# Fourteen of 32 gate panels of a decoder layer moved from between the attention's steps to a stretch of their own ahead of it

## What is computed

```
h    = rmsnorm(x)
proj = h @ w_in          # split into q, kv, nsa_g, u, v, merge_g
o_a  = nsa_attention(q, compressed / selected / window keys and values, sigmoid(nsa_g))
o_b  = spatial_gating(gelu(u), gelu(v), ...)
g    = sigmoid(merge_g)                        # 2 x 2048 columns
merged = g[0] * (o_a @ w_proj_a) + g[1] * (o_b @ w_proj_b)
x    = x + merged @ w_mix_out
```

## Time and profile before

| | us |
|---|---|
| median of 2 runs | 2777.32 |
| lowest and highest | 2776.36, 2778.28 |
| span of the profiled execution | 2772.1 |
| first product of `sv` in it | 810.28 |

### The profile page before, as it was taken

The page is one execution under the profiler, slowest core; times in us unless marked ns, Lnnn a source line. Parts: engine busy times, 40 slices in busy tenths (PEclk is TensorE's granted clock), DMA queues, the critical chain, the costliest instruction groups (busy, mean ns, idle before and its releaser), DMA issues.

```text
span 2772.1 us, 37764 instructions
## 1 busy us (share of the span) xinstructions
PE 2737.9 (99%) x14015; PEld 2313.9 (83%) x14015; DVE 2050.9 (74%) x3133; ACT 1083.8 (39%) x1831; POOL 442.5 (16%) x406
## 2 busy tenths in 40 slices
PE   8999999999999999999999999999999999999998
PEld 7888788888888888888877888888888888788886
DVE  7544476776655555555678899999999999988887
ACT  6201254444420322211144555555555555443334
POOL 0200133343320445511000000000000000010000
PEclk9999999999999999999999999999999999999999
DMA  8532323322233444544334788888888888899882
GB/s 248 165 93 74 86 77 96 96 77 81 80 110 91 108 135 136 155 114 114 110 115 127 187 198 213 213 205 211 208 219 201 215 198 260 290 307 302 289 269 95
DMA packets 610806, 455.19 MB, mean 164 GB/s; under 512 B 13669, under 2 KB 555225, under 8 KB 604761
## 3 DMA queue, kind: packets, MB, share of 16 engines
q1 hardware_dynamic: 551328, 405.97, 49.3%
q0 software_dynamic: 46416, 30.41, 8.2%
q10 hardware_dynamic: 12904, 16.71, 1.9%
HBM read 394.06 MB, written 58.98 MB: 163 GB/s over the span
## 4 chain that ended last, share of the span: by engine, by line
PE 85%; DVE 6%; ACT 3%; issue 2%; DMA 2%; POOL 1%; ACTq 0%; DVEq 0%; SPq 0%; POOLq 0%
PE banks L893 12%; PE banks L894 12%; PE banks L895 12%; PE banks L1293 9%; PE banks L1290 9%; PE banks L1291 9%; PE banks L1355 4%; PE banks L1357 4%; PE banks L1356 4%; PE banks L1062 1%; PE banks L1121 1%; PE banks L1123 1%; PE banks L1122 1%; PE banks L1093 1%; PE banks L1078 1%
## 5 line engine op out<-in xcount | busy, mean ns | idle before, releaser
L1372 DVE CAST w_hi<-raw 128x512 fp32r<-128x512 f32 x424 | 229.1, 540 | 357.6 <-PE banks L895 292.7
L893 PE MATMUL banks<-act_hi,w_hi 128*128 128x512 f32 (+1 forms) x1232 | 489.3, 397 | 0.0
L894 PE MATMUL banks<-act_lo,w_hi 128*128 128x512 f32 (+1 forms) x1232 | 481.1, 390 | 0.0
L895 PE MATMUL banks<-act_hi,w_lo 128*128 128x512 f32 (+1 forms) x1232 | 481.0, 390 | 0.0
L1374 DVE TENSOR_TENSOR w_lo<-raw,w_hi 128x512 fp32r<-128x512 f32 x424 | 314.2, 741 | 14.6
L1291 PEld LDWEIGHTS banks<-t_hl,wf_lo 128*128 128x128 f32 x1312 | 246.5, 188 | 58.3
L895 PEld LDWEIGHTS banks<-act_hi,w_lo 128*128 128x128 f32 (+1 forms) x1232 | 230.2, 187 | 51.3
L893 PEld LDWEIGHTS banks<-act_hi,w_hi 128*128 128x128 f32 (+1 forms) x1232 | 230.7, 187 | 40.7 <-DVE w_lo L1374 0.6
L894 PEld LDWEIGHTS banks<-act_lo,w_hi 128*128 128x128 f32 (+1 forms) x1232 | 230.9, 187 | 39.4
L1293 PE MATMUL banks<-t_hl,wf_hi 128*128 128x512 f32 x656 | 259.4, 396 | 0.0
L1290 PE MATMUL banks<-t_hl,wf_hi 128*128 128x512 f32 x656 | 259.2, 395 | 0.0
(11 more groups left out here) (323 smaller groups left out, 5351.8 us busy)
## 6 DMA issues: line engine op xcount, KB each, us to landing
raw_f<-in_w_ffn_in_dram SPq DMA_DIRECT2D x82, 1024.0 KB, 8.9
raw<-in_w_in_dram SPq DMA_DIRECT2D x68, 1024.0 KB, 5.6
h_full<-hidden_blocks SPq DMA_DIRECT2D x35, 1024.0 KB, 8.1
wo_raw<-in_w_ffn_out_dram SPq DMA_DIRECT2D x32, 1024.0 KB, 10.1
hidden_blocks<-tok_hl SPq DMA_DIRECT2D x44, 512.0 KB, 6.2
s<-in_w_ffn_in_dram SPq DMA_DIRECT2D x40, 512.0 KB, 5.9
s<-in_w_ffn_in_dram POOLq DMA_DIRECT2D x40, 512.0 KB, 6.5
raw<-in_w_mix_out_dram SPq DMA_DIRECT2D x16, 1024.0 KB, 6.1
```

Of the source, the lines that this page charges most:

```text
L893: pe.matmul(dst, w_hi[:, q, j, 0:m], hi, start=first, stop=False)
L894: pe.matmul(dst, w_hi[:, q, j, 0:m], lo, start=False, stop=False)
L895: return pe.matmul(dst, w_lo[:, q, j, 0:m], hi, start=False, stop=last)
L1372: dve.tensor_copy(w_hi[:, q, :, 0:width], src).then_inc(hi_done, 1)
```

## The change

`plan()` gets a phase `m0` of 14 panels between `g` and `merge`, and `merge` keeps 18. PE does the 14 as plain groups, one panel after the other, with `turn_gates` behind the first; DVE splits them whole, with `value_low(3)` behind the first; ACT copies and stores them through the same two buffers `gate_out`. The planner now spreads 288 tiles over the same 128 steps: 38, 83, 68, 77 and 22. The order of the panels, of the stores and of all phases behind stays.

```diff
+EARLY_GATES = 14
...
-        ("merge", (32,)), ("sv", (8,)), ("su", (8,)), ("ab", (16, 4, 2, 2)), ("wo", (16,)),
+        ("m0", (EARLY_GATES,)), ("merge", (2 * DK - EARLY_GATES,)), ("sv", (8,)), ("su", (8,)), ("ab", (16, 4, 2, 2)), ("wo", (16,)),
...
-        GATE_TILES = 32 * DK
+        GATE_TILES = PH["merge"].n * DK
...
-            columns(PH["merge"], w_in_v, C_MERGE)
+            columns(PH["m0"], w_in_v, C_MERGE)
+            columns(PH["merge"], w_in_v, C_MERGE + EARLY_GATES * P)
...
+            ph = PH["m0"]
+            for n in range(ph.n):
+                group(ph, *ph.at(n), hi16, lo16)
+                if n == 0:
+                    turn_gates()
+
             ph = PH["merge"]
             def gate_tiles(tiles):
...
                 gate_tiles(tiles[:third])
-                if step == 0:
-                    turn_gates()
                 if step < ITEMS:
                     scores(step)
...
+            ph = PH["m0"]
+            for n in range(ph.n):
+                split(ph, *ph.at(n))
+                if n == 0:
+                    value_low(3)
             ph = PH["merge"]
             split(ph, 0, 0, quarters=range(AHEAD))
-            value_low(3)
...
                 for k in QUARTERS_AT[step]:
                     k += AHEAD
-                    split(PH["merge"] if k < 128 else PH["sv"], 0, k % 128 // 4, quarters=(k % 4,))
+                    p = k // 4
+                    if p < PH["merge"].n:
+                        split(PH["merge"], 0, p, quarters=(k % 4,))
+                    else:
+                        split(PH["sv"], 0, 0, quarters=(k % 4,))
...
+            def gates_out(ph, p, tile):
+                act.wait_ge(quarters_done, ph.quarter0 + 4 * p + 4)
+                wait(act, gate_stored[tile % 2], 16 * (tile // 2))
+                act.activation(gate_out[:, tile % 2], bank[(ph.group0 + p) % 2][:], ACT.Copy).then_inc(banks_read, 1)
+                act.wait_ge(banks_read, ph.group0 + p + 1)
+                act.dma_start(merge_dram[tile * P:(tile + 1) * P, :], gate_out[:, tile % 2]).then_inc(gate_stored[tile % 2], 16)
+            for p in range(EARLY_GATES):
+                gates_out(PH["m0"], p, p)
+
             ph = PH["merge"]
...
                     if k % 4 == 3:
-                        p = k // 4
...
+                        gates_out(ph, k // 4, EARLY_GATES + k // 4)
```

## The result

The changed kernel takes 2839.36 us (2838.66 to 2840.07, 2 runs) against 2777.32 us before: a ratio of 1.0228, 95% interval 1.0198 to 1.0257. It is slower; whether by more than 2% is just not certain, since the interval starts at 1.0198. The forecast was 2836 us, in a range of 2823 to 2857. The profiled execution spans 2836.9 us against 2772.1, 64.8 us more.

A forecast was written before the change was run, and what follows sets the result against it. PE's work was taken to bound the kernel before; after the change DVE's loop would make PE stand 59 us, with 0 from the other parts. 2777.3 + 59 = 2836 us, range 2823 to 2857.

The forecast's parts named there:

- The plain stretch: Ahead of the attention, from about 319 us: fourteen panels at 10.84 us each, 152 us at PE's own time.
- Rival D: The plain stretch stalls on loads or the banks' copies: 14 us more, 2850; counted within the sum's 0.80.
- The loop on DVE: In the four scoring windows DVE needs 374.8 us against PE's 315.9, so PE stands 58.9 us.
- The price of a quarter: One weight quarter in DVE's loop: 1.06, say 1.07 us, from steps of 3.75 us with one and 2.69 without.
- the head of the stage: The attention's first three steps, bound by PE: a loss under 1 us.
- the tail: The 28.9 us without scores after the last query block: loses 14 tiles, stays bound by PE, 0 us of loss.
- A: DVE's loop gives way as its waits for ACT shrink: no loss, 2777 us; chance 0.08.
- B: PE is not a step ahead and its chain enters DVE's loop: about 65 us more, 2901; chance 0.06.
- the steps that the prediction had named as the exception: First step of a half in `qi` 1, short for DVE: taken as 0, upper bound 1 us for each of ten halves.
- C: PE's clock falls to 1.2 GHz half of the time in the attention stage: 46 us more, 2882; chance 0.05.

The follow-up runs named there:

- `pe_tiles_first`: The changed kernel with all tiles of a step ahead of its scores, instead of a third each ahead of scores, transposes and weighing: 2849.29 us, ratio 1.0271.

## Why the prediction was right

**What bounds the kernel.** PE's work sets the time before, the change takes none away, so it could not gain. The runs agree: no variant with early panels is under the kernel before.

**The plain stretch.** 152 us at full PE were forecast; 151.6 us with PE full and DVE 41% busy were found. Rival D is out.

**The loop on DVE.** This step carried the sum. Forecast 53.2, 90.0, 105.6 and 126.0 us, 374.8 in all; measured 56.2, 91.6, 103.2 and 128.2, 379.2. The price of a quarter, 1.06 us from two neighbouring steps, and the 1.33 us of wait in the steps of 512 columns came out to the hundredth in the steps shown. The loss over PE's share was forecast as 58.9 us and is 63.3 by the windows. The largest miss by share is `qi` 0: PE stands 10.3 us there for 7.3. DVE still waits 1.19 us for PE's scores at 482 us, and it meets a wait that the kernel before did not have, here in DVE's and ACT's timeline:

```profile
525.05 0.34 ACTq L2158 DMA_DIRECT2D merge_gates<-gate_out  x1
...
525.43 1.31 ACT L2133 ACTIVATE q_hl<-q_t 64x128 fp32r<-64x128 f32 x4 [0.42 <-ACT gate_out L2156]
...
526.11 1.33 DVE L1488 TENSOR_TENSOR q_hl<-q_t,q_hl 64x128 fp32r<-64x128 f32 x4 [0.77 <-ACT q_hl L2133]
```

ACT issues a gate panel's store before it comes to the high part of the next queries, and DVE waits for that; PE's next wait is 2.07 us. In `qi` 2 the loop was 2.4 us shorter than forecast.

**The number.** The forecast missed the median by 3.4 us, which is in part luck. Like for like, by the two profiled executions, the loss is 64.8 us for 59: the loop's 63.3, 2.0 us at the head of the stage, which the prediction had put at under 1, and nearly nothing at the tail. The first median before, to which the 59 us were added, came from two executions and is 2 us above those of the later sets.

**The waits.** DVE's waits for ACT were to stay near 110 us: 100. Its waits for PE near nothing: 5.5. PE's waits were to be near 59 us: the view gives 45.2 without the `gate_out` one. Part of the rest may lie in the way PE's ends are modelled: a matmul of 512 columns shows 0.39 us where the next may start after 0.226, so each of 65 waits can hide up to 0.16 us, by this estimate 10 us at most. Against the 63.3 us of the windows some 8 stay unexplained. The view of ACT's waits was read in part only: ACT also waited 6.3 us for PE's transposes with `prob_c`, which the sum leaves out. Taken off too, they would have made the forecast of the loop worse.

**The rivals.** A fell by the steps themselves. B fell as the main cause by DVE's 5.5 us of waits for PE and by `pe_tiles_first`, though the steps that the prediction had named as the exception, in `qi` 1, were the right ones. C is the one that the prediction took too lightly as a mechanism: it had argued from a window with 13% idle at a clock of 1.00 and from gaps under 1 us, but twelve of PE's waits are over 1 us long, up to 2.07, and behind the longest the clock fell for some 4 us (last section). At fourteen panels that was too short to cost much.

**The chances.** 0.32 stood for within 2% since the sum was only 3.5 us beyond that line. The measured time is beyond it by 6.5 us, and the lower end of its interval, 1.0198, lies on the line.

## What to carry to other kernels

The idle share of an engine that works in order is not its room: add the waits that stand inside its loop, and count as slack only its waits for the engine it serves. Filler work between dependent steps is cover for the bound engine; before moving it out, price what each piece takes from both sides (here 10.84 us of cover for 4.3 us of load a panel), and find from the slack where the first piece starts to cost. If the cover must go, first look at the order inside the loop: one swap on ACT was worth 54 of 62 us.

## What the runs showed of the hardware

The granted clock fell inside the attention, for a short while, once at fourteen panels. Windows of the changed kernel, columns as above, and PE's timeline at the border:

```profile
524.00:530.00 6.00, 3.45 (x20) 2.77 (x21) 4.10 (x17) 3.78 (x13) 3.25 (x6) 0.99 0.12 45
530.00:534.00 4.00, 4.00 (x15) 3.32 (x14) 2.54 (x15) 1.92 (x10) 0.00 (x0) 0.58 0.49 126
534.00:538.00 4.00, 4.00 (x24) 3.38 (x24) 2.77 (x9) 1.10 (x5) 3.17 (x6) 1.00 0.52 136
```

```profile
529.10 0.74 PE L1101 MATMUL banks<-prob_t,v_hl 128*128 128x256 f32 x4 [2.07 <-DVE prob_t L1545]
529.68 0.40 PE L895 MATMUL banks<-act_hi,w_hi 128*128 128x512 f32 x1
...
531.22 0.63 PE L895 MATMUL banks<-act_hi,w_hi 128*128 128x512 f32 x1
531.64 0.63 PE L896 MATMUL banks<-act_lo,w_hi 128*128 128x512 f32 x1
```

Before it fell to the 1.2 GHz level PE had been busy for 3.45 of 6 us, with waits of 1.14 and 2.07 us; then products of 512 columns start 0.42 us apart instead of 0.23, until about 533 us. That is what came before this fall, and not a rule. Later in the same trace PE waits 1.44 us at 816 us and 2.05 us at 821 us, is busy for as little, and the clock stays:

```profile
816.00:822.00 6.00, 3.47 (x20) 2.87 (x21) 4.04 (x10) 1.76 (x4) 0.00 (x0) 1.00 0.47 123
```

In the kernel before every window of the stage is at 1.00. With 18 and 22 panels moved, the mean is 0.96 over the last three blocks and over the whole stage. The Trainium skill, "TensorE: Matmul & The Clock Gate", section "A second HAM failure mode: psum-queue depth-cycling", tells of short, frequent idle times between groups of products with which the clock swings between its levels. The traces agree: the clock falls once with fourteen panels, and with eighteen in the windows of three of the four blocks (0.98, 0.96 and 0.95 after 1.00).
